# Handing x and the memory rows over already turned, and moving memory-norm work behind the weight rounding of the q, k and v projections

## The reference, cut to what matters

```python
def mlstm_layer(x, norm_g, w_in, gate_bias, head_g, w_out, mem_k, mem_v, mq_g, mk_g):
    proj = rms_norm(x, norm_g) @ w_in
    q, k, v, o, ifg, mq = jnp.split(proj, offs, axis=-1)
    ifg = ifg + gate_bias
    hm = mlstm_chunkwise(q, k, v, i_pre, f_pre)
    hm = rms_norm(hm, head_g) * jax.nn.sigmoid(o)
    mo = memory_attention(mq, mem_k, mem_v, mq_g, mk_g)
    return x + jnp.concatenate([hm, mo], axis=-1) @ w_out

def memory_kv(mem, norm_g, w_kv):
    kv = rms_norm(mem, norm_g) @ w_kv
```

## Time and profile before

| what | value |
|---|---|
| median of 3 runs | 1415.05 us (1414.73 to 1415.18) |
| the profiled execution's own time | 1414.58 us |
| its span | 1412.8 us |
| PE busy | 1406.3 us (100%) |
| DVE busy | 1217.8 us (86%) |
| ACT busy | 956.6 us (68%) |
| POOL busy | 99.0 us (7%) |
| DMA moved | 440.97 MB |

### The profile page before, as it was taken

The page is one execution under the profiler, slowest core; times in us unless marked ns, Lnnn a source line. Parts: engine busy times, 40 slices in busy tenths (PEclk is TensorE's granted clock), DMA queues, the critical chain, the costliest instruction groups (busy, mean ns, idle before and its releaser), DMA issues.

```text
span 1412.8 us, 19877 instructions
## 1 busy us (share of the span) xinstructions
PE 1406.3 (100%) x6721; PEld 1180.7 (84%) x6721; DVE 1217.8 (86%) x1186; ACT 956.6 (68%) x840; POOL 99.0 (7%) x147
## 2 busy tenths in 40 slices
PE   9999999999999999999999999999999999999999
PEld 9998888888998888888888888888888888888887
DVE  6486888878776898899999999999998999999887
ACT  7465544444685677777777777777777777777775
POOL 4020000000032020010010000001001000000000
PEclk9999999999999999999999999999999999999999
DMA  9454655554455799999999999999999999999995
GB/s 333 153 182 146 222 196 178 178 199 150 126 179 191 262 375 394 380 376 393 381 383 386 392 361 387 396 384 374 393 378 381 387 394 364 387 394 381 384 393 193
DMA packets 211824, 440.97 MB, mean 312 GB/s; under 512 B 16080, under 2 KB 56468, under 8 KB 211776
## 3 DMA queue, kind: packets, MB, share of 16 engines
q1 hardware_dynamic: 208352, 430.18, 83.3%
q0 software_dynamic: 3408, 10.16, 2.5%
q10 hardware_dynamic: 16, 0.00, 0.0%
HBM read 433.96 MB, written 6.33 MB: 312 GB/s over the span
## 4 chain that ended last, share of the span: by engine, by line
PE 98%; ACT 1%; DVE 1%; issue 0%; POOL 0%; ACTq 0%; DVEq 0%; POOLq 0%
PE PS L1731 21%; PE PS L1732 21%; PE PS L1735 21%; PE PS L1433 5%; PE PS L1434 5%; PE PS L1432 5%; PE PS L1164 3%; PE PS L1220 2%; PE PS L1212 2%; PE PS L1214 2%; PE PS L1271 1%; PE PS L1277 1%; PE PS L1274 1%; PE PS L1720 1%; PE PS L1194 1%; PE PS L1723 1%
## 5 line engine op out<-in xcount | busy, mean ns | idle before, releaser
L1886 DVE TENSOR_TENSOR wlo<-ring,whi 128x2048 fp32r<-128x2048 f32 x334 | 761.1, 2290 | 67.7 <-ACT whi L801 65.6
L801 ACT ACTIVATE whi<-ring 128x2048 fp32r<-128x2048 f32 x334 | 639.8, 1918 | 187.9 <-PE PS L1735 176.9
L1731 PE MATMUL PS<-whi,xhi 128*128 128x512 f32 x864 | 341.2, 395 | 0.0
L1732 PE MATMUL PS<-whi,xlo 128*128 128x512 f32 x864 | 336.5, 389 | 0.0
L1735 PE MATMUL PS<-wlo,xhi 128*128 128x512 f32 x864 | 231.1, 389 | 0.0
L1735 PEld LDWEIGHTS PS<-wlo,xhi 128*128 128x128 f32 x864 | 162.1, 188 | 33.9 <-DVE wlo L1886 0.3
L1731 PEld LDWEIGHTS PS<-whi,xhi 128*128 128x128 f32 x864 | 162.3, 188 | 32.7
L1732 PEld LDWEIGHTS PS<-whi,xlo 128*128 128x128 f32 x864 | 162.4, 188 | 32.2
L1731 PE MATMUL PS<-whi,hhi 128*128 128x512 f32 x440 | 171.4, 390 | 0.0
L1732 PE MATMUL PS<-whi,hlo 128*128 128x512 f32 x440 | 171.2, 389 | 0.0
L1735 PE MATMUL PS<-wlo,hhi 128*128 128x512 f32 x440 | 117.8, 390 | 0.0
(11 more groups left out here) (390 smaller groups left out, 1596.7 us busy)
## 6 DMA issues: line engine op xcount, KB each, us to landing
ring<-in_moe_w_gate_up SPq DMA_DIRECT2D x448, 512.0 KB, 6.8
ring<-in_moe_w_down SPq DMA_DIRECT2D x224, 512.0 KB, 7.1
ring<-in_dense_w_gate_up SPq DMA_DIRECT2D x56, 512.0 KB, 4.5
ring<-in_dense_w_down SPq DMA_DIRECT2D x28, 512.0 KB, 4.3
ring<-in_a_w_in SPq DMA_DIRECT2D x12, 768.0 KB, 7.7
ring<-in_mem_w_kv SPq DMA_DIRECT2D x4, 1024.0 KB, 5.5
ring<-in_a_w_out SPq DMA_DIRECT2D x4, 1024.0 KB, 5.0
ring<-in_b_w_out SPq DMA_DIRECT2D x4, 1024.0 KB, 4.9
```

Of the source, the lines that this page charges most:

```text
L801: nc.scalar.activation(whi[:, j, :], ring[:, h * SLOT:(h + 1) * SLOT], ACT.Copy).then_inc(S("highs"), 1)
L1731: mm(out_, lhsT=xh, rhs=whi[:, j, c0:c0 + HD], start=begin, stop=False)
L1732: mm(out_, lhsT=xl, rhs=whi[:, j, c0:c0 + HD], start=False, stop=False)
L1886: v.tensor_tensor(wlo[:, j, :], ring[:, h * SLOT:(h + 1) * SLOT], whi[:, j, :].bitcast(F32), ALU.subtract).then_inc(S("lows"), 1)
```

## The change

- x and memory come into the kernel a second time, turned (contraction on the partitions). x is loaded turned in four pairs, the first with the `a_norm` gain as eight columns ahead of it (`xTin`), the memory turned in two halves (`memTs`). The plain x and memory are still loaded, for the residual and the norms.
- The first item's weights come packed by partition (`first_weights`); their first half is loaded by ACT's queue, the rest and item 1 by SP's. All the gains come as columns by one DMA of POOL in place of 13, and ACT's gain DMA is gone.
- PE's 32 turns of x and memory and its two turns of gains are gone; it runs 10 warming matmuls in place of 8 and 3.
- SP's order is: turned x pair 0, pair 1, first weights, pair 2, item 1, pair 3, items 2 and 3, plain x, item 4, gate bias, item 5, turned memory, plain memory, positions, router, head gains, then item 6 and on.
- On ACT and DVE the norm of x comes behind rounding of item 3, item 5 is rounded ahead of the gate inputs, item 6 ahead of `qN` (ACT), and all memory work (highs and lows, squares, norm, `mqS`, norm of mq) goes behind item 7 and 9. POOL builds its masks ahead of the memory norm.

SP, before and after:

```diff
-            for part in range(2):
-                w0, view = FIRST[part], stream[0][1][:, 2 * part:2 * part + 2, :]
-                sp.dma_start(ring[:, w0].rearrange("p (k n) -> p k n", k=2), view).then_inc(S("first_in" if part == 0 else f"slot_full{place[0]}"), 16)
-            sp.wait_ge(S("x_in0"), 16)
-            for n in (1, 2):
-                fill_big(place[n], stream[n][1])
+            sp.dma_start(xTin[:, 0:KD + 2 * SEQ], T["x_turned"][:, 0:KD + 2 * SEQ]).then_inc(S("xt_in0"), 16)
+            fill_xt(1)
+            sp.dma_start(ring[:, FIRST[1]], T["first_weights"][:, FIRST[1]]).then_inc(S(f"slot_full{place[0]}"), 16)
+            fill_xt(2)
+            sp.dma_start(ring[:, place[1] * SLOT:place[1] * SLOT + 4 * W0], T["first_weights"][:, 4 * W0:8 * W0]).then_inc(S(f"slot_full{place[1]}"), 16)
+            fill_xt(3)
+            fill_big(place[2], stream[2][1])
+            fill_big(place[3], stream[3][1])
             for t in range(NT):
                 sp.dma_start(xres[:, t], x_d[t * P:(t + 1) * P]).then_inc(S(f"x_in{t}"), 16)
+            fill_big(place[4], stream[4][1])
             gb = T["a_gate_bias"].rearrange("a n -> n a")
...
+            fill_big(place[5], stream[5][1])
+            for half in range(2):
+                ks = slice(half * KH, (half + 1) * KH)
+                sp.dma_start(memTs[:, ks, :], T["mem_turned"][:, ks, :]).then_inc(S(f"memt_in{half}"), 16)
             for t in range(NT):
                 sp.dma_start(memS[:, t], mem_d[t * P:(t + 1) * P]).then_inc(S(f"mem_in{t}"), 16)
-            for n in (3, 4, 5):
-                fill_big(place[n], stream[n][1])
```

DVE and PE:

```diff
+            dve.wait_ge(S("xt_in0"), 16)
+            for k in (0, 1):
+                last = v.tensor_scalar(xhi[:, k, :], xTs[:, k, :], xgain[:, k:k + 1], None, ALU.mult)
             last.then_inc(S("x0_high"), 1)
...
+            first_split_low(3)
+            front_lo(2)
+            front_lo(3)
             norm("x0")
-            front_lo(2)
-            for b in range(4):
-                dve.wait_ge(S("mem_high"), b + 1)
-                v.tensor_tensor(memlo[:, 2 * b:2 * b + 2, :].rearrange("p a s -> p (a s)"), PS[:, b, :],
-                                memhi[:, 2 * b:2 * b + 2, :].rearrange("p a s -> p (a s)").bitcast(F32), ALU.subtract).then_inc(S("mem_low"), 1)
-            norm("mem")
-            front_lo(3)
             front_lo(4)
-            norm("mq0")
+            front_lo(5)
...
-            front_lo(5)
             front_lo(6)
...
             front_lo(7)
+            for half in range(2):
+                dve.wait_ge(S("mem_high"), half + 1)
+                ks = slice(half * KH, (half + 1) * KH)
+                v.tensor_tensor(memlo[:, ks, :], memTs[:, ks, :], memhi[:, ks, :].bitcast(F32), ALU.subtract).then_inc(S("mem_low"), 1)
             front_lo(8)
             values_out(0, (2, 3))
             front_lo(9)
+            norm("mem")
+            norm("mq0")
             dve.wait_ge(S("heads_t"), 2)
...
+            dve.wait_ge(S("gain_in"), 16)
             front_lo(10)
             values_out(1, (0, 1))
             front_lo(11)
```

```diff
-            keep_warm(6, 8)
-            for t in range(NT):
-                pe.wait_ge(S(f"x_in{t}"), 16)
-                for pair in range(4):
-                    last = turn_pair(xres, 2 * pair, t, pair)
...
-            keep_warm(6, 3)
+            keep_warm(6, 10)
             project("gmq", (4, 5), xhi, xlo, "x0")
-            pe.wait_ge(S("gain_in"), 16 * 13)
-            tr(PS[:, 7, 0:NG], grow).then_inc(S("gains_t"), 1)
-            for pair in range(4):
-                for t in range(NT):
-                    pe.wait_ge(S(f"mem_in{t}"), 16)
-                    last = turn_pair(memS, 2 * pair, t, pair)
-                last.then_inc(S("mem_t"), 1)
-            pe.wait_ge(S("gains"), 2)
             project("q", (6, 7), xhi, xlo)
-            pe.wait_ge(S("mem_low"), 4)
             pe.wait_ge(S("gS"), 1)
```

More of the change, by code:

```diff
@@ L605, in _ @@
                                pattern=[[-1, P]], channel_multiplier=1).then_inc(S("ident"), 1)
[L606 to L615, removed]
+            pool.dma_start(gains[:, :], T["gain_columns"]).then_inc(S("gain_in"), 16)
             def rstd_of(name):
@@ L859, in front_hi, with first_split_high @@
                 last.then_inc(S("highs"), 1)
+            def first_split_high(pair):
+                act.wait_ge(S(f"xt_in{pair}"), 16)
+                for k in (2 * pair, 2 * pair + 1):
+                    last = nc.scalar.activation(xhi[:, k, :], xTs[:, k, :], ACT.Copy, scale=xgain[:, k:k + 1])
+                last.then_inc(S("x0_high"), 1)
             def split_high(turned, done, gain_name, turn, bank, pair):
@@ L912, in _ @@
             last.then_inc(S("gS"), 1)
-            front_hi(4)
+            front_hi(5)
+            act.wait_ge(S("gate_raw"), 1)
+            act.wait_ge(S("bias_in"), 32)
+            nc.scalar.activation(gi, PS[0:AH, 3, 0:SEQ], ACT.Identity, bias=bias_i[:, :]).then_inc(S("gate_in"), 1)
+            nc.scalar.activation(gf, PS[0:AH, 3, SEQ:2 * SEQ], ACT.Identity, bias=bias_f[:, :]).then_inc(S("gate_in"), 1)
+            front_hi(6)
+            act.wait_ge(S("through"), through("q.1"))
+            for t in range(NT):
+                last = nc.scalar.activation(qN[:, t], PS[:, 6 + t, 0:aqw], ACT.Copy, scale=rx[:, t:t + 1])
+            last.then_inc(S("qN"), 1)
+            act.wait_ge(S("gate_steps"), 1)
+            nc.scalar.activation(gt, gt, ACT.Exp, scale=-1.0).then_inc(S("gate_in"), 1)
+            act.wait_ge(S("gate_in"), 3)
+            nc.scalar.activation(gt, gt, ACT.Ln, bias=1.0).then_inc(S("gate_in"), 1)
+            front_hi(7)
+            for half in range(2):
+                act.wait_ge(S(f"memt_in{half}"), 16)
+                ks = slice(half * KH, (half + 1) * KH)
+                nc.scalar.activation(memhi[:, ks, :], memTs[:, ks, :], ACT.Copy).then_inc(S("mem_high"), 1)
+            square("mem")
             act.wait_ge(S("sums"), nidx["mem"] + 1)
@@ L919, in _ @@
             square("mq0")
[L920 to L925, removed]
-            for t in range(NT):
[L927 to L934, removed]
             act.wait_ge(S("heads_t"), 1)
+            act.wait_ge(S("mem_low"), 2)
             for b in range(2):
@@ L2079, in _, with first_split_low @@
             v.tensor_copy(identr[:, :], ident[:, :]).then_inc(S("masks_r"), 1)
[L2080 to L2092 removed]
+            dve.wait_ge(S("xt_in0"), 16)
+            for k in (0, 1):
+                last = v.tensor_scalar(xhi[:, k, :], xTs[:, k, :], xgain[:, k:k + 1], None, ALU.mult)
+            last.then_inc(S("x0_high"), 1)
+            def first_split_low(pair):
+                dve.wait_ge(S("x0_high"), pair + 1)
+                for k in (2 * pair, 2 * pair + 1):
+                    last = v.scalar_tensor_tensor(out=xlo[:, k, :], in0=xTs[:, k, :], scalar=xgain[:, k:k + 1],
+                                                  in1=xhi[:, k, :].bitcast(F32), op0=ALU.mult, op1=ALU.subtract)
+                last.then_inc(S("x0_low"), 1)
             for part, (there, done) in enumerate((("first_high", "first_low"), ("highs", "lows"))):
@@ L2507, with gain_columns, of @@
           "moe_router", "moe_w_gate_up", "moe_w_down"]
+def gain_columns(arrays):
+    def of(name, *at):
+        return arrays[f"in_{name}"][at] if at else arrays[f"in_{name}"]
+    mem_q, mem_k = of("mem_q_norm"), of("mem_k_norm")
+    rows = [of("a_norm", 0), of("b_norm", 0), of("kv_norm"), of("mem_norm"), of("ffn_norm"), of("a_head_norm", 0), of("b_q_a_norm", 0),
+            of("kv_a_norm"), *(np.concatenate([g, g]) for g in (mem_q[0], mem_q[1], mem_k[0], mem_k[1])), of("k_head_norm")[0:P], of("b_q_head_norm", 0)[0:P]]
+    return np.ascontiguousarray(np.concatenate([r.reshape(-1, P) for r in rows]).T)
 def kernel(**inputs):
@@ L2519 @@
         views[name] = nc.dram_tensor(f"in_{name}", a.shape, mybir.dt.from_np(a.dtype), kind="ExternalInput").ap()
+    turned = {name: np.ascontiguousarray(arrays[f"in_{name}"][0].reshape(-1, arrays[f"in_{name}"].shape[2] // P, P).transpose(2, 1, 0))
+              for name in ("x", "mem")}
+    columns = gain_columns(arrays)
+    D = turned["x"].shape[1] * P
+    heads, width = arrays["in_a_gate_bias"].shape[1], 4 * arrays["in_mem_q_norm"].shape[1]
+    last = arrays["in_a_w_in"][0][:, -(heads + width):]
+    first = last.reshape(D // P, P, heads + width).transpose(1, 0, 2).reshape(P, -1)
+    x_in = np.concatenate([columns[:, 0:D // P], turned["x"].reshape(P, -1)], axis=1)
+    for name, a in (("x_turned", x_in), ("mem_turned", turned["mem"]), ("gain_columns", columns), ("first_weights", first)):
+        a = np.ascontiguousarray(a)
+        arrays[f"in_{name}"] = a
+        views[name] = nc.dram_tensor(f"in_{name}", a.shape, mybir.dt.from_np(a.dtype), kind="ExternalInput").ap()
     shape = arrays["in_x"].shape
```

57 lines of the change are left out of this document (20 added, 37 removed).

## The result

The changed kernel took 1422.66 us (median of 4, 1421.78 to 1424.51) against 1414.97 before: 7.7 us more, ratio 1.0058 (95% interval 1.0046 to 1.007). It is slower, as forecast, but by half as much again as the 5.1 us of the sum, and it lies 0.16 us over the stated range. The profiled execution took 1424.51, with a span of 1422.6; its time is 9.9 us over that of the kernel before.

A forecast was written before the change was run, and what follows sets the result against it. PE carried 98% of the chain; item 6's later landing (29.7) and ACT's and DVE's written order move memkv0 from 54.12 to 59.2. That 5.1 us on 1414.58 gives 1419.7, forecast 1420.2 us, range 1416.5 to 1422.5.

The forecast's parts named there:

- the sum: Whole kernel: memkv0 starts at 59.2 against 54.12, 5.1 us more, giving 1420.2 us.
- The gain of the start and of the turns: PE up to q: gmq starts 3.1 us earlier, dropped turns save 1.7; 4 to 5 us gained at first.
- item 6's late landing: SP's queue: 2.10 MB added ahead of item 6 costs 5.5 us, so it lands at 29.7 against 24.8.
- `qT`'s wait for the lows: ACT between v0 and v1: qT waits for DVE's memory lows until 43.0, so v1 starts at 45.5, 1.2 us late.
- `values_out(1)` at the end of DVE's: DVE between v1 and memkv0: norms, kT and low 10 in written order end values_out(1) at 59.1, memkv0 starts at 59.2.
- the waits named in advance: PE stands still three times for 1 to 3 us, near 30, 43 and 57 us.
- the one on SP's queue: SP ahead of item 6: six more DMAs cost nothing extra, since item 6 waits in the queue anyway.
- the 24.8 that the sum starts from: Item 6's landing before the change: issued at 18.63, landed 6.2 us later, with DMA engines taken as full.
- The 0.6 us "given back": DMA at 4 to 8 us: packed small weight and gain rows at full rate save 0.23 MB or 0.6 us of the landing.
- The two figures of the Trainium skill: DMA rates: 425 GB/s would land item 6 near 28, sum 1.7 us smaller; 358 near 31.5, 1.8 larger.
- the clock's rival: PE's clock halves behind the last wait; memkv0.0's 5.6 us takes up to twice that, 1425.8 us; chance 0.05 within the slower case.
- PE stays the bound: Moved ACT and DVE work fits their gaps; memkv0 starts at 49.5, 4.6 us gained, 1410.4 us; chance 0.08.

The follow-up runs named there:

- norms late: Changed kernel with only DVE's memory norm and mq norm moved from behind low 9 to behind low 11: 1418.49 us.
- memory split: Changed kernel with only the memory highs (ACT) and lows (DVE) moved ahead of high 6 and low 6: 1418.05 us.
- all of it: Changed kernel with all memory work of ACT and DVE (highs, lows, squares, mqS, both norms) ahead of high 6 and low 6: 1415.10 us.
- small loads late: Changed kernel with SP's positions, router and head gains issued behind items 6 to 9 instead of ahead: 1421.37 us.
- the two kernels with warming matmuls: Changed kernel with 24 warming matmuls on PE ahead of memkv0, 1420.80 us; and with warming in all four waits of PE, 1421.28 us.
- fitted version: Changed kernel, memory highs/lows, Exp, Ln, qN, gate steps before item 6's rounding, norms behind low 11, small loads behind item 9: 1412.96 us; with 24 start warming matmuls 1411.67.
- the one warmed ahead of memkv0: Changed kernel with 24 warming matmuls of 256 columns on PE in its wait for values_out(1): 1420.80 us.
- all four waits filled: Changed kernel with warming matmuls in PE's four waits (20 at start, 16 before qN's turn, 16 before v1, 22 before memkv0): 1421.28 us.
- the fitted version without the warm start: The fitted version with 10 warming matmuls at PE's start, not 24: 1412.96 us.

## Why the prediction was right and wrong

**Right in the mechanism.** The gain of the start and of the turns came at q (2.1 us) and was spent on item 6's late landing; then the memory's work took v1 back by `qT`'s wait for the lows and by ACT's line, and memkv0 by `values_out(1)` at the end of DVE's. Each of the waits named in advance is in the trace. From item 6's landing to memkv0's start I had 29.5 us; it took 29.3. The moves one by one (norms 3.2 us, memory split 3.7, all of it 6.3) show that the order was needed for the loss. The 2.0 for 2.0 of the small loads shows that the landing counts in full behind this order; no run brought it back to 24.8.

**Wrong in the size of the landing.** The step that failed is the one on SP's queue: "SP issues six more DMAs, but item 6 waits in the queue anyway, as its 6.2 us to landing show." In the changed kernel it did not wait in the queue; SP was held 7.1 us at one small load behind the larger ones and issued item 6 at 25.2, when the engines had little left but short rows. That is 2.0 us of the landing (small loads late: 32.0 to 30.0). The 6.2 us to landing could not show it, as they count from the issue on. And "the engines were already full" was read from 24 to 32 us only the earlier trace rows. The kernel before has a hole of the same kind behind its own head gains load, which held SP 4.66 us from 13.45 on (kernel before, columns as in the earlier trace rows):

```profile
19.00:20.00 1.00, 1.00 (x8) 1.00 (x7) 1.00 (x3) 1.00 (x1) 1.00 (x4) 1.00 1.16 197
20.00:21.00 1.00, 1.00 (x8) 1.00 (x7) 1.00 (x2) 1.00 (x4) 0.86 (x2) 1.00 1.08 159
21.00:22.00 1.00, 1.00 (x7) 1.00 (x7) 1.00 (x2) 1.00 (x2) 1.00 (x1) 1.00 0.64 162
```

So the 24.8 that the sum starts from held such a hole already, and the change made it longer. The 0.6 us "given back" did not come either: 4 to 8 us did run faster, 389 GB/s for 323, but 0 to 4 ran at 92 for 188, which is more lost than gained. The two figures of the Trainium skill (DMA: Bandwidth & Descriptors, Bandwidth) had given 28 and 31.5 as estimates; the rows with full engines showed 373 to 407 GB/s, between the two figures, and with SP out of the way the landing of 30.0 lay between the estimates. Neither rate has SP's wait in it, which was as large as their difference from the sum.

**Wrong in keeping the clock out of the sum.** It was a rival at 0.05, with three waits of 1 to 3 us at 30, 43 and 57 us. They were there (2.26, 2.27, 2.58 us, and 0.8 before the last), and the clock was granted at half behind the last of them: 2.6 us in the profiled execution. In the median the two kernels with warming matmuls came out 1.4 and 1.9 us lower, item 6's earlier landing in them included. The Trainium skill (TensorE: Matmul & The Clock Gate, Part 1) had said that it falls when the array idles, and the trace agrees. I gave it little since the trace of before held no such wait, though that row bore on neither side. The price of up to 5.6 us was too high, as only some thirteen matmuls of memkv0 ran at half.

**The start** came at 6.39 and not at 4.9: I had taken both first landings at 4.22 us from a load of another shape on one queue, and they came at 5.4 and 5.7. That is 1.5 of the 2.3 us by which q was later than forecast. The rest arose in gmq, where the clock was granted at half from 8.9 to 12.3 us, behind a wait that the clock's rival had not named. It cost nothing in the changed kernel, where PE waited at `qN` anyway; in the fitted version it is what is left to gain.

**Small errors of the sum.** q and k take 8.43 and 8.44 us by the earlier trace rows (17.07 to 25.50, 25.85 to 34.29) and not 8.3, and the gates' turn 0.35 and not 0.5: k's end is 29.8. The gain at k's end is 4.5 us by 17.07 to 12.6, and not 4.9. The estimates of 28 and 31.5 come to 27.4 and 31.0 when the 21.7 us from the eighth microsecond on are scaled from 380 GB/s. None of this moves the forecast, since in it item 6's landing set the pace and not k's end.

In the sum: 5.1 forecast, 2.0 more at memkv0 by the landing (2.2 late, less 0.2 behind it), 2.6 more by the clock, 9.8 in the profiled execution's span. The median lies 1.9 below that execution's time. Of the rivals, "PE stays the bound" is what the fitted version makes true, with its memkv0 at 51.1 against the 49.5 that I had named.

## What to carry to other kernels

A transfer that seems to wait in the queue anyway should be checked at its issue: small many-row loads ahead of it can hold the issuing engine until the large ones have drained, so they belong behind the loads with a near due time. Where the first deep prefetch is bound by bandwidth, inputs handed over in a second layout are paid for in the landing of everything behind them, and work that used to stand in a slack must be placed in the new wait, ahead of the item that is late. And every new wait of PE should be priced twice, once as itself and once as a clock that may be halved behind it: waits of 2.3 to 2.7 us brought it down in some executions here and not in others. Spare matmuls in the waits took the second price away, but too many of them are a wait of their own.

## What the runs showed of the hardware that was not expected

- SP's issue of one 96 KB load of 128 rows took 7.10 us with large loads outstanding ahead of it (4.66 before the change), and the DMA engines had fallen to 94 GB/s just behind it, and to 159 before the change.
- Two first loads of some 260 KB on two queues landed after 4.6 and 4.9 us; the same first load with SP's queue alone after 3.6, and the first 512 KB in the kernel before, where a second 512 KB was issued right behind, after 3.3.
- The granted clock fell behind one wait or another of like length, differently from execution to execution: from 60 to 67 us in the changed kernel, from 47.3 to 50.7 in the one warmed ahead of memkv0, from 35.9 to 39.3 with the memory split early. With all four waits filled it stayed at 1.00.
- gmq's matmuls of 264 columns started up to 0.22 us apart from about 9 to 12 us, behind the wait of 1.5 us at the start, and 0.12 to 0.14 later. In the changed kernel the record grants half the clock for that stretch; in norms late and in the fitted version without the warm start it grants 1.00 throughout, at the same spacing.
